# Expert layers on one core: nine blocks of dots ahead of the gates' spread, and one-hot columns of GpSimd that carry the gate

## The reference, cut to what matters

```python
def peer(x, w_q, keys, u_tab, v_tab):
    q = _f(xt @ w_q).reshape(n, PK_HEADS, 2, PK_HALF)
    s = jnp.einsum('thcd,hcnd->thcn', q, _f(keys))
    sv, si = lax.top_k(s, PK_TOPK)
    cand = (sv[:, :, 0, :, None] + sv[:, :, 1, None, :]).reshape(n, PK_HEADS, PK_TOPK * PK_TOPK)
    best, bi = lax.top_k(cand, PK_TOPK)
    i1 = jnp.take_along_axis(si[:, :, 0], bi // PK_TOPK, axis=-1)
    i2 = jnp.take_along_axis(si[:, :, 1], bi % PK_TOPK, axis=-1)
    eidx = i1 * N_KEYS + i2
    gate = jax.nn.softmax(best, axis=-1)
    act = jax.nn.gelu(_f(jnp.einsum('td,ted->te', xi, u_tab[ei]))) * gi
    return jnp.einsum('te,ted->td', act.astype(xi.dtype), v_tab[ei])
```

## Time and profile before

| | us |
|---|---|
| median of 3 runs | 4286.23 |
| lowest and highest | 4280.3, 4286.56 |
| the profiled execution's own time | 4284.1 |
| its span, first to last instruction | 4282.3 |
| TensorE busy (matmul) | 3884.7 (91%) |
| VectorE busy | 3038.4 (71%) |
| GpSimd busy | 1910.2 (45%) |
| ScalarE busy | 688.4 (16%) |

### The profile page before, as it was taken

The page is one execution under the profiler, slowest core; times in us unless marked ns, Lnnn a source line. Parts: engine busy times, 40 slices in busy tenths (PEclk is TensorE's granted clock), DMA queues, the critical chain, the costliest instruction groups (busy, mean ns, idle before and its releaser), DMA issues. The chain is left out here.

```text
span 4282.3 us, 46161 instructions
## 1 busy us (share of the span) xinstructions
PE 3884.7 (91%) x16342; PEld 2307.9 (54%) x16342; DVE 3038.4 (71%) x6236; ACT 688.4 (16%) x1432; POOL 1910.2 (45%) x1654
## 2 busy tenths in 40 slices
PE   7986899997999899999979997999888999999897
PEld 3643656775444444444447875577744444444442
DVE  6747635888877777778763146588988777777787
ACT  4122511163000000000023122103600000000000
POOL 0002300077777677776700000003867767677673
PEclk9997899998999999999989999999999999999999
DMA  4212741269999999999922105013899999999996
GB/s 178 89 50 99 280 170 40 72 180 340 411 415 420 420 419 419 418 416 417 419 92 68 59 20 128 20 55 119 270 408 403 420 420 420 420 419 417 416 418 259
DMA packets 375715, 1169.31 MB, mean 273 GB/s; under 512 B 35833, under 2 KB 120281, under 8 KB 364042
## 3 DMA queue, kind: packets, MB, share of 16 engines
q0 software_dynamic: 184960, 679.58, 39.1%
q1 hardware_dynamic: 107856, 445.02, 27.5%
q10 hardware_dynamic: 82684, 41.95, 3.5%
HBM read 1116.99 MB, written 48.37 MB: 272 GB/s over the span
## 5 line engine op out<-in xcount | busy, mean ns | idle before, releaser
L608 PE MATMUL banks<-h_dense_T,blocks 128*128 128x320 f32 x4096 | 1139.1, 432 | 0.0
L656 PE MATMUL banks<-blocks,picked_T 128*128 128x512 f32 x2048 | 989.6, 627 | 0.0
L608 PEld LDWEIGHTS banks<-h_dense_T,blocks 128*128 128x128 f32 x4096 | 776.9, 190 | 387.3 <-issue 98.5
L427 POOL DMA_INDIRECT expert_rows<-in_pk_u_dram,expert x640 | 820.4, 1282 | 346.9 <-DVE own_dots L913 164.8
L938 DVE SCALAR_TENSOR_TENSOR acc<-expert_rows,expert_weight,acc 128x1024 f32<-128x1024 f32 x628 | 794.6, 1284 | 253.1 <-DMA expert_rows<-in_pk_v_dram,expert 248.0
L427 POOL DMA_INDIRECT expert_rows<-in_pk_v_dram,expert x640 | 817.3, 1277 | 327.1 <-issue 158.8
L913 DVE CUSTOM_DVE_ANT_0 expert_rows<-expert_rows,h_rows 128x1024 f32<-128x1024 f32 x640 | 773.8, 1225 | 248.3 <-DMA expert_rows<-in_pk_u_dram,expert 243.8
L656 PEld LDWEIGHTS banks<-blocks,picked_T 128*128 128x128 f32 x2048 | 384.9, 198 | 619.8 <-issue 619.8
L647 PE MATMUL banks<-blocks,picked_T 128*64 128x512 f32 x1024 | 297.1, 657 | 195.3 <-DVE picked_T L899 194.7
L451 ACT ACTIVATE dense_act<-banks 128x320 f32<-128x320 f32 x246 | 107.8, 438 | 2107.4 <-PE banks L608 2107.4
L415 POOL TENSOR_SCALAR expert_rows<-iota,picked_T 128x128 f32<-128x128 f32 x320 | 207.0, 664 | 440.0 <-ACT picked_T L457 394.4
(11 more groups left out here) (528 smaller groups left out, 3908.1 us busy)
## 6 DMA issues: line engine op xcount, KB each, us to landing
blocks<-in_pk_u_turned_dram SPq DMA_DIRECT2D x256, 512.0 KB, 6.5
blocks<-in_pk_v_dram SPq DMA_DIRECT2D x256, 512.0 KB, 6.5
ada_block<-in_ada_rest_dram SPq DMA_DIRECT2D x32, 1280.0 KB, 6.9
gates_dram<-shared ACTq DMA_DIRECT2D x40, 1024.0 KB, 5.5
shared<-gates_dram SPq DMA_DIRECT2D x32, 1280.0 KB, 10.5
blocks<-in_pk_w_q_dram SPq DMA_DIRECT2D x32, 512.0 KB, 3.5
expert_rows<-in_pk_u_dram,expert POOLq DMA_INDIRECT x640, 13.0
expert_rows<-in_pk_v_dram,expert POOLq DMA_INDIRECT x640, 13.3
```

The costliest lines, as they stand in the source:

```text
L427: pool.indirect_dma_start(out=rows[:, r % RING, :], out_offset=None, in_=table, in_offset=bass.IndirectOffsetOnAxis(ap=idx[:, at_:at_ + 1] ...
L608: mm = pe.matmul(dense_dots(c), u[:, k * P:(k + 1) * P], HT[:, k, 0:DENSE], start=(k == 0), stop=(k == KD - 1))
L656: mm = pe.matmul(ps[:, at_:at_ + HALF], wt[:, c % WEIGHED, z * P:(z + 1) * P], v[:, half_ * HALF:(half_ + 1) * HALF], start=(c == 0), stop ...
```

## The change

Three things. The dots are placed anew: 9 blocks before the spread in place of 16 (`EARLY`), 8 in its gaps in place of 5 (`GAPS`), and so 8 after it in place of 4; the 25 in all stay, as do `EXTRA` and the rooms that hang on it. ScalarE's exponentials stand before the gelus of blocks 2, 4 and 6. And in GpSimd's 40 groups a layer the gate moves from one factor to the other: GpSimd's compare now also multiplies by the gate, and VectorE makes these groups' `second_hot` as plain compares, four tokens with one instruction, in the form of line 884. The 40 groups of ScalarE and VectorE stay as they were.

```diff
-GAPS = (7, 14, 21, 28, 35)
-EXTRA = len(GAPS)
+GAPS = (4, 9, 13, 17, 21, 25, 29, 33)
+EXTRA = 5
...
-EARLY = (0, 9, 13, 16)
-MIDDLE = EARLY[-1] + EXTRA
+EARLY = (0, 5, 7, 9)
+EXPS_AT = (2, 4, 6)
+MIDDLE = EARLY[-1] + len(GAPS)
...
                     pool.tensor_scalar(hot(first_hot, n), iota128[:],
-                                       cols[:, z, 0, t:t + 1], None, ALU.is_equal
-                                       ).then_inc(hot_first, 1)
+                                       cols[:, z, 0, t:t + 1], cols[:, z, 2, t:t + 1],
+                                       ALU.is_equal, ALU.mult).then_inc(hot_first, 1)
...
             for z in range(ND):
-                if z:
-                    exponentials(z)
                 for c in range(EARLY[z], EARLY[z + 1]):
-                    if c == 6:
-                        exponentials(0)
+                    if c in EXPS_AT:
+                        exponentials(EXPS_AT.index(c))
                     gelu(c)
                 columns(z)
...
+                    if maker(n // 4) == "P":
+                        if n % 4 == 0:
+                            dve.tensor_tensor(hot(second_hot, n, 4),
+                                              iota128[:, :].unsqueeze(1).to_broadcast([P, 4, P]),
+                                              cols[:, z, 1, t:t + 4].unsqueeze(2).to_broadcast(
+                                                  [P, 4, P]), ALU.is_equal).then_inc(hot_second, 4)
+                        continue
                     dve.tensor_scalar(hot(second_hot, n), iota128[:],
                                       cols[:, z, 1, t:t + 1], cols[:, z, 2, t:t + 1],
                                       ALU.is_equal, ALU.mult).then_inc(hot_second, 1)
```

## The result

| | before | after |
|---|---|---|
| median | 4284.69 (4 runs) | 4330.61 (4 runs) |
| lowest and highest | 4280.3, 4286.56 | 4325.51, 4345.96 |
| profiled execution, its own time | 4284.1 | 4325.51 |
| its span | 4282.3 | 4323.7 |

The ratio is 1.0112, with a 95% interval from 1.0096 to 1.0127: 46 us slower, where 18 were forecast.

The account below looks back on a forecast made before the run. GpSimd was taken to bound the spread, the full DMA the rest. Per layer 3.9 us later plus 5.0 of moved bytes, 17.8 for both layers, on 4286.2 gave 4304; range 4272 to 4370.

Parts of the forecast that it names:

- Start of the spread: Layer 0: with VectorE's 8.5 us of waits for exponentials gone, the spread starts at about 876.5, 18 us earlier.
- Which engine bounds the spread: In the spread of the gates, GpSimd is the limit even with its new operation free, ending it at 991.4.
- TensorE's floor of 108.6 us: TensorE's work in the spread: 74.1 us of small products and 34.5 of eight blocks; no end before 985.7.
- The hold-up by VectorE's compares: In the spread, some 50 added four-token compares each hold GpSimd up by 0.48 us, 24 us in all.
- GpSimd's new scalar: Second operation and scalar in GpSimd's compare: 0.07 us on each of 144 columns, 10.1 us; spread ends at 1001.5.
- the bounds of 0 and 0.30: Price of the second scalar on GpSimd's column: at least nothing, at most 0.30 us, as much as the first.
- rival 3: GpSimd's second scalar costs as much as the first, 0.30 us: 4370, or 4341 at 0.2; chance 0.15.
- the border of the range: The forecast's own range, for a GpSimd scalar of 0.04 to 0.15 us, is 4294 to 4330.
- the 3.4 of ring waits: GpSimd's waits for its ring once the spread runs, 3.4 us, counted into its end at 990.1.
- The moved bytes: After the spread, four more block loads fall where the DMA is full: 2.1 MB, 5.0 us a layer.
- The gates' loads: In SyncE's queue they wait behind block loads, but gates land in DRAM only 26 us after the spread: nothing added.
- The two rules cited: For GpSimd's compare: two operations bound by the port, end 991.4; scalar as small read command, 0.085 us, end 1003.6.

Follow-up runs that it names:

- experiment 1: Changed kernel with the one-hots of before, so only dots and exponentials are placed anew: 4285.38 against 4287.47, ratio 0.9995.
- experiment 5: Changed kernel with VectorE's four-token compares of GpSimd's groups made as four one-token compares: 4321.84, ratio 1.0084 to before.
- experiment 6: Two kernels on the placement of experiment 1, with another form of GpSimd's column for each token of a group; only GpSimd's pace was read.
- experiment 7: Kernel before with one block of dots in the spread in place of five, so eight follow it: 4286.75 against 4285.07, ratio 1.0004.
- experiment 3: Changed kernel with GpSimd's compare in its old form of one operation, leaving out its groups' gates: 4278.64, ratio 0.9988 to before.

## Why the prediction was right and wrong

**Start of the spread:** right. 876.5 forecast, 876.28 measured; VectorE's 8.5 us of waits for the exponentials are gone, and TensorE now waits for VectorE (4.29 and 3.41 us before the transposes).

**Which engine bounds the spread:** right, GpSimd, in one run of 144 columns. TensorE's floor of 108.6 us was confirmed by experiment 1 with 109.2.

**The hold-up by VectorE's compares:** forecast 24 us, measured 21.1 in the changed kernel (132.37 - 111.3) and 21.6 with one operation. The size is about right. The reason given, compares with two inputs alone, is too narrow: one-token compares also hold up the column with two scalars (experiments 5 and 6).

**GpSimd's new scalar:** this is the step that failed. The prediction took 0.07 us for the whole new form, priced the second scalar by VectorE's 0.061 and the multiply at nothing. The scalar costs 0.079, near what was taken. The multiply costs 0.117 and is paid by the element. The row that was to show it free is a multiply with an add, a form that takes 0.284 us at this size where a compare with a multiply takes 0.616 (experiment 6). The true 0.196 lies inside the bounds of 0 and 0.30 and near the 0.2 at which rival 3 has 4341, 10 above the measured 4331, but the forecast and the border of the range leant on the wrong row. (By the prediction's own sum a scalar of 0.15 us gives 4327 and one of 0.04 gives 4295, not quite the 4330 and 4294 written down.)

In numbers: 144 x (0.196 - 0.07) = 18.1 us more a layer; less 2.9 of hold-up and the 3.4 of ring waits that vanish when GpSimd is never ahead, and 0.7 for its later restart at 880.31: 1001.5 + 18.1 - 2.9 - 3.4 + 0.7 = 1014.0, measured 1013.7. Counted from the first dots, which came 0.9 us earlier than in the profile of before, the first gather is 17.0 us later than before in layer 0 and 18.3 in layer 1, where 3.9 were forecast: 27.5 us more for both, and the time is 28 us further from before than forecast (46 against 18).

**The moved bytes:** the size was right, 9.7 against 10.0 for both layers, and right that filling TensorE's wait before the first sums gains nothing (experiment 7). The gates' loads were not "nothing added": they came 4.7 us later after the spread's end (30.8 against 26.1), beside the block loads. TensorE so waited 5.42 us for the first sums instead of starting them right behind the 25th block. No cost of its own shows in the sum, and the DMA is full there.

**The two rules cited.** The Trainium skill, GPSIMD Engine Reference, section on side-by-side cycle accounting, has bodies of up to two operations an element bound by the port. The traces agree for multiply with add (0.284 us for 128 columns, 1.05 for 1024). They don't for a compare with a multiply, which costs 0.11 to 0.12 us more than the compare alone at 128 columns and half of that at 64, and the measurement decides. The estimate of 0.085 us from the Trainium skill's figure for a small read command (same page, section on pitfalls for Q7 kernels) is near the 0.08 of a second scalar from memory at 64 and at 128 columns; that the scalar is such a command no run shows.

## What to carry to other kernels

Price an added operation by a row of the same pair of operations on the same engine, and a price that may hang on the element by two sizes: on GpSimd two forms of one instruction, of the same size, differ by more than a factor of two. When work moves from one engine to another, look at what the receiver does per instruction (144 x 0.196 us here) before counting what the giver saves, and at the third engine that stands right behind both: with GpSimd relieved (experiment 3), TensorE bounded the same stage at once. And filling TensorE's wait ahead of the stretch bound by DMA gained nothing here; what counted was when the stretch started and how many bytes were left for it.

## What the runs showed of the hardware that was not expected

- VectorE's one-token compares hold up some forms of GpSimd's column and not others: 0.506 becomes 0.559 (compare, one number), 0.693 becomes 0.741 and 0.773 becomes 0.825 (compare and multiply with one and with two scalars from memory), while 0.577 (compare, one scalar), 0.616 (compare and multiply, two numbers) and 0.284 (multiply and add) stay. Neither the number of operations nor that of scalars sorts them; why is open.
- On GpSimd a multiply behind a compare is paid by the element (0.057 us on 64 columns, 0.116 on 128), a second scalar from memory by the instruction (0.08 to 0.09 on either).
- Multiply with add on GpSimd is as fast as 0.284 us for 128 columns; a compare with one scalar takes twice that, although it is one operation less.
- TensorE's granted clock in the spread fell to a mean of 0.93 in the changed kernel, where it waited often, against 1.00 before; the small products took 291 ns in place of 277 on the page's mean. With GpSimd as the bound this cost nothing visible.
